# A three-block network on one core: two row homes for the scan, weights split in place, and the weight load waits for the matmuls

## The chip, the cores and the metric

The kernel runs on one core of a Trainium2 chip. Its time is the device time of one execution in microseconds (us). Before the change three timed runs gave 2862.00, 2860.92 and 2841.12 us (median 2860.92 us), and the one profiled execution took 2826.98 us with a span of 2825.3 us.

## The reference, cut to what matters

One sequence of 512 tokens, width 1024, float32, goes through two layers of a first block and one of a second:

```python
x = layer_norm(ALPHA * x + even_mixer(x)); x = layer_norm(ALPHA * x + conv_ffn(x))   # retention + stick-breaking
x = layer_norm(ALPHA * x + odd_mixer(x));  x = layer_norm(ALPHA * x + conv_ffn(x))   # differential attention
x = x + hybrid_mixer(rms_norm(x))             # SSD scan + windowed attention, gated
x = x + memory_cross_attention(rms_norm(x), rms_norm(mem))
x = x + swiglu_ffn(rms_norm(x)); return rms_norm(x)
...
def ssd_chunked(xh, dt, a_head, b_in, c_in):  # the scan, here for both directions and 32 heads
    a_cum = cumsum(dt * a_head)
    decay = exp(where(lower, a_cum[:, :, :, None] - a_cum[:, :, None], -inf))
    cb = einsum('bclgn,bcsgn->bclsg', c_c, b_c)
    y_diag = einsum('bclsg,bclsgr,bcsgrp->bclgrp', cb, decay, x_c)
    ... # plus what earlier chunks hand on
```

The kernel computes the scan as full 512 by 512 products: for each head the decay weights exp(row - column) times C·B, times the tokens.

## The kernel before, in words

**Weights.** All weight matrices lie in memory as one stream of 405 units, each 128 partitions of 8 blocks of 128 float32 (512 KB). Every matmul of a weight is done in three parts for accuracy: high part of the weight by high and low part of the activation, low part of the weight by the high one. One unit is 48 matmuls of 256 columns in `product_tile` (L338), or the same work in `half_tile` (L369) and the memory products (L1467). A unit passes through a ring of four slots (RING = 4) in three tensors. SP loads it into `w_raw` (`load_unit`, L305). ScalarE copies it into `w_hi`, which rounds (`split_hi`, L313). VectorE writes `w_lo` = `w_raw` - `w_hi` (`split_lo`, L319). Unit u uses slot u mod 4. PE waits for `lo_done` and counts `units_used` when it is done with a unit. `split_hi` of unit u+4 waits for `units_used` of unit u. The load of unit u+4 waits only for `lo_done` of unit u, since `w_raw` is then free: the raw copy lies ready long before PE gives the slot back.

**The engines' order.** Every engine runs its program in the order written. ScalarE's program says, tile for tile: wait until PE is done with the tile, evict it from PSUM, then `split_hi` of the unit four ahead. VectorE likewise has its `split_lo` between evictions and norms. Nothing reorders this when a wait is long. PSUM has two banks for product tiles (`acc`), so PE can start a tile only when the tile two before it is evicted.

**The scan** (`ssd_pe`, `ssd_act`, `ssd_dve`, `ssd_rows_dma`; stage `ssd`). 16 head tiles f, in 4 groups g of 4 (j = 0 to 3). For a tile PE computes two product tiles (gate and x, L338), then the heads of the tile before (L1731, L1734: 16 matmuls with the decay weights as the moving side), then transposes of x (L1769). At j = 0 it also makes C·B (L1752), at j = 1 a sum of squares (L1740). The decay weights of two heads (b = 0, 1) are 5 slots of 2 KB each: GpSimd fills them from `scratch_rows` by eight broadcast DMAs of 320 KB (L1710), one per chunk c and head, each after PE is done with that chunk of the previous tile (`s_pv`). VectorE caps a chunk (L1867), ScalarE takes the exponentials (L1842), VectorE multiplies by C·B (L1872), PE uses it. There is one home of 10 slots for these rows, so tile f+1's rows start only after tile f's heads. ScalarE waits for the transposes before it starts on the exponentials (L1831 ahead of L1842), and VectorE does both `split_lo` and the output (L1879, L1882) before the first cap.

**Layer norms beside matmuls.** After `even_out`, `down0` and `odd_out` the norm is done in halves of 256 columns: while PE does the last tiles in halves (L369), ScalarE's `tail_act` first does one `split_hi` and then the squares (L460), whose sum PE takes (L453). In other places a stage's end is: evict the last tile, `split_hi`, then the work on which PE waits (copies of transposes L677, L1152, L2051, the last square L1327, the high parts L2220).

## Time and profile before

| | |
|---|---|
| timed runs | 2862.00, 2860.92, 2841.12 us (median 2860.92) |
| the profiled execution's own time | 2826.98 us |
| its span | 2825.3 us |
| PE busy | 2647.1 us (94%) |
| VectorE busy | 1453.8 us (51%) |
| ScalarE busy | 1244.8 us (44%) |
| scan, the stretch from 1540 to 1870 us | 330 us |

A busy time is the time in which an engine had an instruction under way. It is an average over stages with different limits, so the windows by stage and the waits tell more than the shares. The chain of waits is followed back from the last instruction. A number in brackets behind an instruction is the idle time of its engine just before it, and what ended it. Matmul records overlap, since matmuls are pipelined.

### The profile page before, as it was taken

The page shows a single profiled execution, that of the slowest core. Times are in us where ns is not written, and L with a number is a line of the kernel's source. Part 1 is how long each engine was busy: PE and PEld are TensorE (multiplying, and loading weights), DVE is VectorE, ACT ScalarE, POOL GpSimd, SP SyncE. Part 2 cuts the span into 40 slices and gives each one's busy share as a digit, 9 for nine tenths or more (in the row PEclk, how much of TensorE's full clock was granted, in tenths as well). Part 3 has the DMA queues.
Part 4 walks back from the last instruction along what each step waited for, and adds up shares of the span by engine and source line. Part 5 has one row for each costly group of instructions (what it writes and reads, how often), then busy time and mean ns, then how long its engine had stood idle before and what let it go on. Part 6 is the DMA issues. An engine that isn't in the chain of part 4 may idle for free.

```text
span 2825.3 us, 52535 instructions
## 1 busy us (share of the span) xinstructions
PE 2647.1 (94%) x20916; PEld 2429.6 (86%) x20916; DVE 1453.8 (51%) x2514; ACT 1244.8 (44%) x2045; POOL 83.5 (3%) x157
## 2 busy tenths in 40 slices
PE   7998999999998699999988999889988998999998
PEld 7985899999996399999987776679966986899998
DVE  3233476553424766664466777752376343433333
ACT  3335354432425644442355777752465234333321
POOL 0000000000000000000001211200000000000000
PEclk9999999999999999999999999999999999999999
DMA  6310122222321022223253454532211231222231
GB/s 181 123 67 0 45 90 89 95 98 99 112 97 53 1 75 99 95 98 119 98 187 117 169 197 156 186 123 98 89 46 53 97 105 45 75 97 97 97 105 68
DMA packets 74693, 278.20 MB, mean 98 GB/s; under 512 B 9642, under 2 KB 9674, under 8 KB 74048
## 3 DMA queue, kind: packets, MB, share of 16 engines
q1 hardware_dynamic: 60816, 217.42, 22.4%
q0 software_dynamic: 13744, 58.88, 6.8%
q8 instruction: 98, 1.61, 0.2%
q14 instruction: 35, 0.29, 0.0%
HBM read 267.03 MB, written 9.24 MB: 98 GB/s over the span
## 4 chain that ended last, share of the span: by engine, by line
PE 79%; DVE 9%; ACT 5%; DMA 4%; issue 3%; DVEq 0%; ACTq 0%; POOL 0%; POOLq 0%; SPq 0%
PE acc L338 66%; PE acc L369 2%; DMA res_tmp<-scratch_rows 2%; PE ps L813 1%; DMA w_raw<-in_stream 1%; PE ps L369 1%; PE acc L1467 1%; ACT w_hi L313 1%; PE ps L453 1%; DVE big L2173 1%; DVE big L1276 1%; PE ps L1740 1%; PE acc L827 1%; DVE res_tmp L1872 1%; DVE res_tmp L1358 1%
## 5 line engine op out<-in xcount | busy, mean ns | idle before, releaser
L338 PE MATMUL acc<-x_split,w_hi 128*128 128x256 f32 x7968 | 1254.6, 280 | 23.6 <-DVE x_split L1363 12.0
L338 PEld LDWEIGHTS acc<-x_split,w_hi 128*128 128x128 f32 x7968 | 1072.3, 190 | 28.6 <-issue 22.2
L319 DVE TENSOR_TENSOR w_lo<-w_raw,w_hi 128x1024 fp32r<-128x1024 f32 x405 | 493.1, 1222 | 605.9 <-ACT w_hi L313 605.9
L338 PE MATMUL acc<-x_split,w_lo 128*128 128x256 f32 x3984 | 786.3, 279 | 0.0
L313 ACT ACTIVATE w_hi<-w_raw 128x1024 fp32r<-128x1024 f32 x405 | 424.9, 1054 | 578.8 <-PE acc L338 527.2
L338 PEld LDWEIGHTS acc<-x_split,w_lo 128*128 128x128 f32 x3984 | 609.1, 190 | 0.0
L338 PE MATMUL acc<-big_r,w_hi 128*128 128x256 f32 x3560 | 559.0, 279 | 7.7 <-DVE big_r L2226 3.4
L338 PEld LDWEIGHTS acc<-big_r,w_hi 128*128 128x128 f32 x3560 | 477.5, 188 | 9.8 <-issue 3.6
L338 PE MATMUL acc<-big_r,w_lo 128*128 128x256 f32 x1780 | 351.7, 279 | 0.0
L338 PEld LDWEIGHTS acc<-big_r,w_lo 128*128 128x128 f32 x1780 | 271.6, 189 | 0.0
L1842 ACT ACTIVATE res_tmp<-res_tmp 128x512 f32<-128x512 f32 (+3 forms) x256 | 120.7, 550 | 43.4 <-DVE res_tmp L1867 42.9
L958 ACT ACTIVATE res_tmp<-acc,par 128x512 f32<-128x512 f32 x84 | 64.8, 772 | 143.0 <-PE acc L338 138.5
L983 DVE SCALAR_TENSOR_TENSOR res_tmp<-acc,par,res_tmp 128x511 f32<-128x511 f32 x84 | 62.9, 748 | 93.5 <-ACT res_tmp L958 93.2
L1872 DVE TENSOR_TENSOR res_tmp<-res_tmp 128x640 f32<-128x640 f32 x128 | 99.0, 819 | 6.6 <-ACT res_tmp L1842 5.9
L1602 DVE SCALAR_TENSOR_TENSOR big<-acc,par,big 128x510 f32<-128x510 f32 (+3 forms) x96 | 71.9, 749 | 37.7 <-ACT big L1592 27.9
L1710 POOL DMA_DIRECT2D res_tmp<-scratch_rows x128 | 68.7, 537 | 295.4 <-PE ps L1734 227.0
L986 DVE SCALAR_TENSOR_TENSOR res_tmp<-acc,par,res_tmp 128x510 f32<-128x510 f32 x84 | 62.9, 748 | 13.1 <-DVE res_tmp L983 3.1
L963 ACT ACTIVATE res_tmp<-res_tmp 128x512 f32<-128x512 f32 x44 | 27.8, 633 | 89.5 <-DVE small L991 89.5
L1120 ACT ACTIVATE big<-acc 128x512 f32 (+1 forms) x30 | 18.0, 599 | 109.5 <-PE acc L338 107.1
L369 PE MATMUL acc<-big_r,w_hi 128*128 128x256 f32 x344 | 61.9, 283 | 0.5 <-DVE res_tmp L533 0.5
L1867 DVE TENSOR_TENSOR res_tmp<-res_tmp 128x512 f32<-128x512 f32 x64 | 43.3, 687 | 31.9 <-DMA res_tmp<-scratch_rows 31.9
L1731 PE MATMUL ps<-res_tmp,big 128*64 128x512 f32 (+3 forms) x256 | 48.2, 455 | 10.3 <-DVE res_tmp L1872 10.1
(291 smaller groups left out, 2579.1 us busy)
## 6 DMA issues: line engine op xcount, KB each, us to landing
w_raw<-in_stream SPq DMA_DIRECT2D x405, 512.0 KB, 3.3
res_tmp<-scratch_rows POOLq DMA_DIRECT2D x128, 320.0 KB, 5.7
scratch_bias<-res_tmp POOLq DMA_DIRECT2D x1, 2560.0 KB, 55.3
res_tmp<-in_x SPq DMA_DIRECT2D x2, 1024.0 KB, 7.7
res_tmp<-scratch_bias POOLq DMA_DIRECT2D x8, 256.0 KB, 4.4
scratch_x<-res_tmp POOLq DMA_DIRECT2D x1, 2048.0 KB, 8.1
scratch_kv<-big POOLq DMA_DIRECT2D x1, 2048.0 KB, 8.7
res_tmp<-scratch_x POOLq DMA_DIRECT2D x1, 2048.0 KB, 8.5
```

What stands on the lines that cost most here:

```text
L313: act.activation(w_hi[:, u.slot], w_raw[:, u.slot], ACT.Copy).then_inc(hi_done, 1)
L319: dve.tensor_tensor(w_lo[:, u.slot], w_raw[:, u.slot], w_hi[:, u.slot].bitcast(F32), ALU.subtract).then_inc(lo_done, 1)
L338: mm = pe.matmul(a[:, h], w, AR[:, x + k, h], start=(k == 0 and w is wh and x == hi and h.start == 0), stop=(k == total - 1 and w is wl), ...
L369: mm = pe.matmul(a[:, cols], w, AR[:, x + k, cols], start=(start and k == 0 and w is wh and x == hi), stop=(k == total - 1 and w is wl), s ...
L958: act.activation(x, acc[t.bank][:], ACT.Identity, bias=col(f"cb{f}", tile), scale=col(f"cw{f}", tile + 88)).then_inc(ev("conv_now"), 1)
L983: dve.scalar_tensor_tensor(x[:, 1:S], a[:, 0:S - 1], col(f"cw{f}", tile + 44), x[:, 1:S], ALU.mult, ALU.add).then_inc(ev("conv_tap1"), 1)
L986: dve.scalar_tensor_tensor(x[:, 2:S], a[:, 0:S - 2], col(f"cw{f}", tile), x[:, 2:S], ALU.mult, ALU.add).then_inc(acc_free[t.bank], 1)
L1602: ins = dve.scalar_tensor_tensor(o, i, col("cw2", m + 24 * j), o, ALU.mult, ALU.add)
L1710: pool.dma_start(part(b, c), src).then_inc(ev(f"s_row_in{b}{c}"), 16)
L1731: pe.matmul(o(b, c * P, S), x(b, c), rows_buf(b)[:, FORE[c]:FORE[c] + LEN[c]], start=(c == 0), stop=False, skip_group_check=True)
L1842: ins = act.activation(x, x, ACT.Exp, bias=tab[:, 0, c, ds(head, 1)])
L1872: dve.tensor_tensor(w, w, cb, ALU.mult).then_inc(ev("s_w"), 1)
```

## The change

Three things change together.

1. `w_raw` is given the address of `w_lo`: VectorE's subtraction writes the low part over the raw unit. So the load of unit u+4 may no longer start when the low part of unit u is made; it waits for `units_used`, that is until PE is done with unit u. The three ring tensors of 16 KB each per partition become two. The arena before them grows from 76 to 84 slots of 2 KB, by just the 16 KB, so `w_hi` and `w_lo` keep their addresses.
2. The scan's rows get two homes of 10 slots (`rows_buf(p, b)`), for even and odd tiles, and `s_pv` starts 8 higher: the rows of tile f+2 are loaded when the heads of tile f are done, chunk by chunk.
3. Inside the scan VectorE caps the first two chunks before the output of the tile before, and spreads the two `split_lo` and the `times_cb` between the other caps. ScalarE starts the exponentials at once and copies the transposed x (L1831) after the first two chunks.

```diff
-RES = 60
-TMP = 68
-N_SLOTS = 76
+RES = 64
+TMP = 72
+N_SLOTS = 84
...
-        w_raw = ctx.enter_context(nc.sbuf_tensor("w_raw", [P, RING, BLK * P], F32))
         w_hi = ctx.enter_context(nc.sbuf_tensor("w_hi", [P, RING, BLK * P], F32R))
+
+        home = nc.sbuf_base
         w_lo = ctx.enter_context(nc.sbuf_tensor("w_lo", [P, RING, BLK * P], F32R))
+        w_raw = nc.alloc_sbuf_tensor_at("w_raw", [P, RING, BLK * P], F32, offset=home)
...
         def load_unit(sp, u, wait=True):
             if wait:
-                sp.wait_ge(lo_done, (u + (-RING)).count + 1)
+                sp.wait_ge(units_used, (u + (-RING)).count + 1)
...
             def body(i):
-                for c in range(CH):
-                    for b in range(2):
-                        pool.wait_ge(ev("s_pv"), 8 * i + (2 * c + b + 1))
-                        src = SCR_ROWS[ds(2 * i + b, 1), BACK[c]:BACK[c] + S + P].to_broadcast([P, S + P])
-                        pool.dma_start(part(b, c), src).then_inc(ev(f"s_row_in{b}{c}"), 16)
-            repeat(pool, SSD_TILES, body)
+                for p in range(2):
+                    for c in range(CH):
+                        for b in range(2):
+                            pool.wait_ge(ev("s_pv"), 16 * i + (8 * p + 2 * c + b + 1))
+                            src = SCR_ROWS[ds(4 * i + (2 * p + b), 1), BACK[c]:BACK[c] + S + P].to_broadcast([P, S + P])
+                            pool.dma_start(part(p, b, c), src).then_inc(ev(f"s_row_in{p}{c}"), 16)
+            repeat(pool, SSD_TILES // 2, body)
...
-                    act.wait_ge(ev("s_xtt"), f + 1)
-                    act.activation(A[:, XTOK + j % 2], ps[:, 2], ACT.Copy).then_inc(ev("s_xtok"), 1)
                     table_of_exp_and_ln(act)
                     if j == 1 and not first:
                         rstd(g + (-1))
                     for c in range(CH):
+                        if c == 2:
+                            act.wait_ge(ev("s_xtt"), f + 1)
+                            act.activation(A[:, XTOK + j % 2], ps[:, 2], ACT.Copy).then_inc(ev("s_xtok"), 1)
...
-            dve.memset(small[:, 41:42], 0.0).then_inc(ev("s_pv"), 2 * CH)
+            dve.memset(small[:, 41:42], 0.0).then_inc(ev("s_pv"), 4 * CH)
...
+                    cap(g, j, 0)
+                    cap(g, j, 1)
+                    if j or not first:
+                        out(4 * g + (j - 1), (j - 1) % 4)
                     split_lo(dve, uz + RING)
-                    split_lo(dve, uz + 1 + RING)
...
+                    cap(g, j, 2)
+                    times_cb(f, j, 0)
+                    split_lo(dve, uz + 1 + RING)
+                    cap(g, j, 3)
+                    times_cb(f, j, 1)
...
+                    times_cb(f, j, 2)
+                    times_cb(f, j, 3)
```

Lines below the ring tensors move: L305 becomes L307, L313 L315, L319 L321, L1602 L1606, L1867 L1873, L1872 L1879, L1879 L1886, L1882 L1889, L1831 L1841 and L1842 L1848.

**SP's queue, the loop that loads the stream**, with the semaphore that each row waits for. Before:

```order
L305 ISA [waits w_lo_done]
L305 DMA w_raw<-in_stream 128x1024
L302 REGISTER_ALU
L305 ISA [waits w_lo_done]
L305 DMA w_raw<-in_stream 128x1024
```

Now:

```order
L307 ISA [waits w_units_used]
L307 DMA w_raw<-in_stream 128x1024
L304 REGISTER_ALU
L307 ISA [waits w_units_used]
L307 DMA w_raw<-in_stream 128x1024
```

Nothing moves in this queue; each load waits for the matmuls in place of the subtraction.

**VectorE, one tile of the scan** (second tile of the first group, from its convolution to the next one's; `big` are the arena's lower slots, `res_tmp` its upper ones). Before:

```order
L1602 SCALAR_TENSOR_TENSOR big<-acc,par,big 128x510
L319 TENSOR_TENSOR w_lo<-w_raw,w_hi 128x1024 x2
L1879 SCALAR_TENSOR_TENSOR big<-big,par,ps 128x512
L1882 TENSOR_TENSOR big<-big 128x512
L1867 TENSOR_TENSOR res_tmp<-res_tmp 128x2x256 x2
L1872 TENSOR_TENSOR res_tmp<-res_tmp 128x640 x2
L1867 TENSOR_TENSOR res_tmp<-res_tmp 128x2x256
L1872 TENSOR_TENSOR res_tmp<-res_tmp 128x640 x2
L1867 TENSOR_TENSOR res_tmp<-res_tmp 128x2x256
L1872 TENSOR_TENSOR res_tmp<-res_tmp 128x640 x4
```

Now:

```order
L1606 SCALAR_TENSOR_TENSOR big<-acc,par,big 128x510
L1873 TENSOR_TENSOR res_tmp<-res_tmp,big 128x2x256 x2
L1886 SCALAR_TENSOR_TENSOR big<-big,par,ps 128x512
L1889 TENSOR_TENSOR big<-big 128x512
L321 TENSOR_TENSOR w_lo<-w_raw,w_hi 128x1024
L1873 TENSOR_TENSOR res_tmp<-res_tmp,big 128x2x256
L1879 TENSOR_TENSOR res_tmp<-res_tmp,big 128x640 x2
L321 TENSOR_TENSOR w_lo<-w_raw,w_hi 128x1024
L1873 TENSOR_TENSOR res_tmp<-res_tmp,big 128x2x256
L1879 TENSOR_TENSOR res_tmp<-res_tmp,big 128x640 x6
```

The same instructions in number: two caps stand ahead of the output, and the second low part stands behind the first products with C·B.

**ScalarE, the same tile.** Before:

```order
L1592 ACTIVATE big<-acc,par 128x512
L1821 ACT_TABLE_LOAD
L1821 ACTIVATE big<-acc 128x512
L313 ACTIVATE w_hi<-w_raw 128x1024 x2
L1827 ACTIVATE big<-big 128x512
L1831 ACTIVATE big<-ps 128x512
L285 ACT_TABLE_LOAD
L1842 ACTIVATE res_tmp<-res_tmp 128x512
```

Now:

```order
L1596 ACTIVATE big<-acc,par 128x512
L1826 ACT_TABLE_LOAD
L1826 ACTIVATE big<-acc 128x512
L315 ACTIVATE w_hi<-w_raw 128x1024 x2
L1832 ACTIVATE big<-big 128x512
L287 ACT_TABLE_LOAD
L1848 ACTIVATE res_tmp<-res_tmp,big 128x512
```

The copy of the transposed x (L1831) has gone from between the activation of x and the exponentials; it now stands eight exponentials later. The two `split_hi` stay where they were, ahead of the activation of x (L1827) for which PE's transposes wait.

## Rows read from the trace of the kernel before

**Rows 1.** The page: span, and PE's busy time with its share.

```profile
span 2825.3 us, 52535 instructions
PE 2647.1 (94%) x20916; PEld 2429.6 (86%) x20916; DVE 1453.8 (51%) x2514; ACT 1244.8 (44%) x2045; POOL 83.5 (3%) x157
```

**Rows 2.** The scan's stretch: busy us of PE, PEld, DVE, ACT, POOL; clock, DMA share, GB/s.

```profile
1540.00:1870.00 330.00, 289.13 (x2080) 226.59 (x2078) 263.40 (x376) 257.01 (x446) 67.34 (x126) 0.94 0.52 178
```

**Rows 3.** Waits in the scan, 1540 to 1871: us in total, times, longest.

```profile
DVE res_tmp L1867 <- DMA res_tmp<-scratch_rows: 31.9, 21, 3.2
PE ps L1769 <- ACT big L1827: 25.6, 13, 3.4
```

**Rows 4.** The chain of waits, 1763 to 1803: start, us, what.

```profile
1769.39 11.09 PE acc L338 x96
1780.48 3.43 PE ps L1752 x8
...
1790.81 9.45 DMA res_tmp<-scratch_rows
```

**Rows 5.** Instructions of PE in order of time, 1762 to 1781: start, us, engine, line.

```profile
1763.34 1.08 PE L1731 MATMUL ps<-res_tmp,big 128*64 128x512 f32 x4
...
1768.74 0.66 PE L1769 MATMUL ps<-const,big 128*128 128x128 f32 x4 [0.87 <-ACT big L1827]
```

**Rows 6.** Instructions of VectorE in order of time, 1822 to 1885.

```profile
1827.93 3.43 DVE L1602 SCALAR_TENSOR_TENSOR big<-acc,par,big 128x510 f32<-128x510 f32 x4 [0.44 <-ACT big L1592]
...
1846.83 3.43 DVE L1602 SCALAR_TENSOR_TENSOR big<-acc,par,big 128x510 f32<-128x510 f32 x4
```

**Rows 7.** The page's groups: the two splits; busy us, mean ns; idle before, releaser.

```profile
L319 DVE TENSOR_TENSOR w_lo<-w_raw,w_hi 128x1024 fp32r<-128x1024 f32 x405 | 493.1, 1222 | 605.9 <-ACT w_hi L313 605.9
...
L313 ACT ACTIVATE w_hi<-w_raw 128x1024 fp32r<-128x1024 f32 x405 | 424.9, 1054 | 578.8 <-PE acc L338 527.2
```

**Rows 8.** The page's DMA issues: count, KB each, median us to landing.

```profile
w_raw<-in_stream SPq DMA_DIRECT2D x405, 512.0 KB, 3.3
...
scratch_bias<-res_tmp POOLq DMA_DIRECT2D x1, 2560.0 KB, 55.3
```

**Rows 9.** The weight loads issued in 34 to 60 us: issues, and time to landing.

```profile
L305 SPq DMA_DIRECT2D w_raw<-in_stream x4: 332/333/333, 39.6 to 55.8; - x4
...
DMA to landing us min/median/max: 22.8/26.0/27.8
```

**Rows 10.** Instructions of ScalarE in order of time, 20 to 90.

```profile
51.27 0.60 ACT L623 ACTIVATE res_tmp<-acc 64x512 f32<-64x512 f32 x1 [3.15 <-PE acc L338]
...
62.45 1.06 ACT L313 ACTIVATE w_hi<-w_raw 128x1024 fp32r<-128x1024 f32 x1 [4.54 <-DMA w_raw<-in_stream]
...
69.92 1.06 ACT L313 ACTIVATE w_hi<-w_raw 128x1024 fp32r<-128x1024 f32 x1 [5.18 <-DMA w_raw<-in_stream]
```

**Rows 11.** Instructions of ScalarE at stage ends, 184 to 190 and 2441 to 2446.

```profile
184.80 1.05 ACT L313 ACTIVATE w_hi<-w_raw 128x1024 fp32r<-128x1024 f32 x1
185.74 4.01 ACT L677 ACTIVATE big<-ps 128x512 f32<-128x512 f32 x8
...
2444.02 1.06 ACT L313 ACTIVATE w_hi<-w_raw 128x1024 fp32r<-128x1024 f32 x1 [4.07 <-PE acc L338]
```

**Rows 12.** ScalarE in the norm after `even_out`, 342 to 351.

```profile
342.64 1.06 ACT L313 ACTIVATE w_hi<-w_raw 128x1024 fp32r<-128x1024 f32 x1 [12.20 <-PE acc L369]
343.90 2.73 ACT L460 ACTIVATE res_tmp<-res_tmp 128x256 f32<-128x256 f32 x8 [0.20 <-DVE res_tmp L478]
```

**Rows 13.** VectorE at the end of `even_out`, 328 to 334.

```profile
329.18 1.23 DVE L319 TENSOR_TENSOR w_lo<-w_raw,w_hi 128x1024 fp32r<-128x1024 f32 x1 [0.47 <-ACT w_hi L313]
...
333.33 0.41 DVE L533 SCALAR_TENSOR_TENSOR res_tmp<-res_tmp,acc 128x256 f32<-128x256 f32 x1
```

**Rows 14.** VectorE in `up1`, one pair of tiles, 1127 to 1134.

```profile
1127.21 1.22 DVE L319 TENSOR_TENSOR w_lo<-w_raw,w_hi 128x1024 fp32r<-128x1024 f32 x1
...
1132.42 0.75 DVE L986 SCALAR_TENSOR_TENSOR res_tmp<-acc,par,res_tmp 128x510 f32<-128x510 f32 x1
```

More of the change, by code:

```diff
@@ L1624, in bcdt_act @@
             act.activation(d, d, ACT.Ln).then_inc(ev("s_logdt"), 1)
-            rows = rows_buf(0)
+            rows = rows_buf(0, 0)
             act.wait_ge(ev("s_rows"), 8)
@@ L1668, in bcdt_dve @@
             split_lo(dve, u + RING)
-            rows = rows_buf(0)
+            rows = rows_buf(0, 0)
             dve.wait_ge(ev("s_ones"), 1)
@@ L1696, in ssd_rows_dma @@
         def ssd_rows_dma(pool):
-            rows = rows_buf(0)
+            rows = rows_buf(0, 0)
             pool.wait_ge(ev("s_rows"), 8)
@@ L1853, in ssd_dve, with cap @@
             dve.wait_ge(ev("s_tab"), 2)
-            dve.memset(small[:, 41:42], 0.0).then_inc(ev("s_pv"), 2 * CH)
+            dve.memset(small[:, 41:42], 0.0).then_inc(ev("s_pv"), 4 * CH)
             dve.memset(small[:, 42:43], 0.0).then_inc(ev("s_w"), 1)
-            def cap(f, head, c):
-                for b in range(2):
-                    dve.wait_ge(ev(f"s_row_in{b}{c}"), 16 * (f + 1))
-                x = A[:, ROWS:ROWS + 10].rearrange("p (b m) n -> p b (m n)", b=2)
+            def cap(g, j, c):
+                p, head = j % 2, g * 8 + 2 * j
+                dve.wait_ge(ev(f"s_row_in{p}{c}"), 64 * g + 32 * (j // 2 + 1))
+                x = A[:, ROWS + 10 * p:ROWS + 10 * p + 10].rearrange("p (b m) n -> p b (m n)", b=2)
                 x = x[:, :, (S + 2 * P) * c:(S + 2 * P) * c + 2 * P].rearrange("p b (k n) -> p b k n", k=2)
@@ L1867, in cap, with times_cb @@
                 dve.tensor_tensor(x, x, own, ALU.min).then_inc(ev("s_cap"), 1)
-            def times_cb(f, b, c):
-                dve.wait_ge(ev("s_e"), 8 * f + (2 * c + b + 1))
-                w, cb = part(b, c), cb_packed[:, BACK[c]:BACK[c] + S + P]
-                dve.tensor_tensor(w, w, cb, ALU.mult).then_inc(ev("s_w"), 1)
+            def times_cb(f, j, c):
+                for b in range(2):
+                    dve.wait_ge(ev("s_e"), 8 * f + (2 * c + b + 1))
+                    w, cb = part(j % 2, b, c), cb_packed[:, BACK[c]:BACK[c] + S + P]
+                    dve.tensor_tensor(w, w, cb, ALU.mult).then_inc(ev("s_w"), 1)
             def out(f, j):
                 v = A.at(VL, f)
-                dve.wait_ge(ev("s_pv"), 8 * f + 4 * CH)
+                dve.wait_ge(ev("s_pv"), 8 * f + 6 * CH)
                 dve.wait_ge(ev("s_xt"), f + 1)
@@ L1910, in group @@
                     uz, tz = Units(UB["ssd"] + 2 * j, g, 8), Tiles(TB["ssd"] + 2 * j, g, 8)
-                    x = A[:, XT + j % 2]
-                    conv5_dve(dve, tz + 1, f + 8, f + 8, x)
+                    conv5_dve(dve, tz + 1, f + 8, f + 8, A[:, XT + j % 2])
                     if j == 0:
                         table_diagonals(g)
+                    cap(g, j, 0)
+                    cap(g, j, 1)
+                    if j or not first:
+                        out(4 * g + (j - 1), (j - 1) % 4)
                     split_lo(dve, uz + RING)
-                    split_lo(dve, uz + 1 + RING)
                     if j == 2 and not first:
                         scaled(g + (-1))
-                    if j or not first:
-                        out(4 * g + (j - 1), (j - 1) % 4)
                     if j == 0:
@@ L1923, in group @@
                         dve.wait_ge(ev("s_cb_rest"), 4 * g + 4)
+                    cap(g, j, 2)
[3 more added lines that the diff above has]
+                    times_cb(f, j, 1)
                     if j == 3 and not first:
                         lows(g + (-1))
-                    for c in range(CH + 1):
-                        if c < CH:
-                            cap(f, g * 8 + 2 * j, c)
-                        if c:
-                            times_cb(f, 0, c - 1)
-                            times_cb(f, 1, c - 1)
+                    times_cb(f, j, 2)
+                    times_cb(f, j, 3)
             group(0, True)
@@ L1953, in gated_act @@
             if not first:
-                act.wait_ge(ev("s_pv"), 2 * CH * (SSD_TILES + 1))
+                act.wait_ge(ev("s_pv"), 2 * CH * (SSD_TILES + 2))
             per = 1 + len(blocks)
```

19 lines of the change are left out of this document (10 added, 9 removed).

## The prediction

> **What bounds the kernel now.** I read the page first: PE is busy 94% of a span of 2825.3 us [rows 1], so on the whole time goes only when PE stops, and the three other engines matter where they make it stop. Next the stretch of the scan, because the change names it: there PE is busy 289 of 330 us, at 0.94 of the full clock, while VectorE has 263 and ScalarE 257 us of work [rows 2]. So 41 us of PE's idle time lie there, and no other engine is near its limit on average. The waits say who makes the others idle: VectorE's cap waited 31.9 us for the decay rows, and PE's transposes waited 25.6 us in 13 waits for ScalarE's activation of x [rows 3]. The chain of waits shows the loop: products of 11.09 us, C·B of 3.43 us, then the heads, and after these 9.45 us of row DMA before VectorE may start [rows 4]. With one home the rows of a tile can't come before the heads of the tile before.
>
> Then I looked at what hides the weight loads. The raw copy lands 3.3 us after issue in the median [rows 8]. The splits take 1.05 and 1.22 us, and the page's rows say for whom they waited: `w_hi` in 527.2 of its 578.8 us for PE, to give the slot back; its waits for a load are too small to be named first [rows 7]. The reader is to see in this that ScalarE stands at PE's heels: at stage ends `split_hi` starts at once behind the eviction, and the next work of ScalarE starts at once behind it [rows 11].
>
> **The change part by part.** The sum is made against the profiled execution.
>
> *Nothing by itself:* no instruction is added to PE, VectorE or ScalarE. The arena grows by 16 KB, just what the third ring tensor took, so the weights that PE reads stand at the same addresses. Writing the low part over the raw unit is the same instruction, and I see no row by which an equal output address costs; it is read and written by one engine in step. I price it at 0.
>
> *The rows in two homes.* Their DMA (9.45 us in the chain) goes behind a whole tile of other work: it starts with the heads of tile f and is wanted 17 us later. What is late next? PE's own tile: 11.09 us of products [rows 4], then from the first head at 1763.34 to the end of the transposes at 1768.74 + 0.66 is 6.06 us, with 0.87 us of waiting in it for ScalarE [rows 5]. That is 17.15 us a tile; a group of four has 3.43 us of C·B and as much for the sum of squares on top: 4 x 17.15 + 6.9 = 75.5 us. VectorE, which ran without a gap there, took 1846.83 - 1827.93 = 18.9 us for a tile in which it scales a group, and has about as much in the tile with the low parts [rows 6]; the new order puts no work away, so in two tiles of four it holds PE up by about 1 us each. So 77.5 us a group, 310 us for four against 330 us: **-20 us**. Bounds: at best all 41 us of idle time and a clock back from 0.94 (some 14 us more), -55 us; at worst the second `split_hi` of each tile waits for a load whose slot was given back only 2.6 us earlier, 16 tiles at 1 to 2 us, and half of the gain is gone: -5 us. I take the middle since the floor comes from rows of this very loop.
>
> *The load waits for PE.* From "PE done with unit u" to "raw copy of u+4 there" now pass the 3.3 us of [rows 8] and some 0.2 us for SP, 3.5 us in place of nothing. In a plain stage that is hidden: a unit takes PE 5.4 us, the slot is wanted again after three units (16 us), and 3.5 + 1.05 + 1.22 us fit. But ScalarE now stands in `split_hi` for up to 3.5 us with everything behind it queued, and VectorE behind ScalarE in `split_lo`. I went through each stage end:
> - Four times the copies of transposed tiles stand behind the last `split_hi` of a stage (184.8, 878.1, 2074.6 and 2354.7). The slot came free 0.6 us before the split started, so each is 2.9 us later [rows 11]: 4 x 2.9 = 11.6 us.
> - Two rms norms (2300.3 and 2444.0) have the last square behind a `split_hi` that starts at once when PE stops [rows 11]: 2 x 3.5 = 7 us.
> - Before `mix_out`, before `bcdt` and within it (2251.4, 1463.2, 1474) the split stands ahead of high parts, low parts and scans: 3.2 + 3.2 + 1.5 = 7.9 us.
> - The halved norms. At the end of `even_out` VectorE's split at 329.18 stands ahead of the half tile's eviction at 333.33, and PE waited for that one already [rows 13]: 3.5 us. Then `split_hi` at 342.64 stands ahead of the squares at 343.90, which PE takes as they come [rows 12]: the load lands at 346.1, the split ends at 347.1, 3.2 us later. `odd_out` is the same code, `down0` has only the second: 2 x 6.7 + 3.1 = 16.5 us.
> - The cross attention's keys (`xkv`) are half as wide, 2.8 us a unit, between two norms, and a 2 MB store runs beside them. ScalarE is often 2 to 5 us behind there, which hides part: 5 us, between 0 and 10.
>
> Together **+48 us**. The lower bound: where a load lands while ScalarE is late anyway, it costs nothing; half of it, 24 us. Above: each new stop of PE may be followed by a stretch at a lower clock, as the scan's 0.94 shows for its stops, 1 us at 12 places, 60 us.
>
> *The start.* Early in the first stage a DMA of 2560 KB is under way for 55.3 us [rows 8], and four weight loads issued from 39.6 to 55.8 us took 22.8 to 27.8 us [rows 9]. Before, that was covered, since units 4 to 7 had been loaded ahead of it: of ScalarE's waits for loads of 4.5 and 5.2 us [rows 10] PE felt about 2 us. Now unit 4 is asked for when PE is done with unit 0, at about 35 us (51.27 us is the fourth tile's eviction, 5.44 us a tile back), and lands at 35 + 22.8 = 58 us. Meanwhile ScalarE stands in `split_hi`, the second tile isn't evicted, and PE stops after the third, at 46 us, until 61 us. The next loads land 69.92 - 62.45 = 7.5 us apart [rows 10], slower than PE's 5.44 us, until the DMA is over; by then PE is at unit 7 at 94 us. Unit 9 ends at 105 us in place of 35 + 9 x 5.44 + 2 = 86 us: **+19 us**.
>
> Weighed against this: the Trainium skill (DMA: Bandwidth & Descriptors, Queues, rings and completion order) says that a DMA engine goes round robin between its queues, packet by packet. By that a load would pass the big DMA at every second packet and come in perhaps 8 us, and the start would cost 3 us, the sum be 16 us less. The trace disagrees for the first load (22.8 us with nothing ahead of it in its own queue) and is nearer to it for the next (7.5 us apart). I go by the rows and keep 3 us as the lower bound; the upper one is 26 us, with 27.8 us for the first landing.
>
> The same skill page (Rules for kernel authors) advises to issue a DMA early and wait for it late, since its fixed cost is then hidden. It speaks against this change: the load is issued as late as it can be. That is the +48 us above, which rests on the rows and not on the rule.
>
> *A margin to watch.* In `up0` and `up1` a pair's second split ends, and 1132.42 + 0.75 - (1127.21 + 1.22) = 4.7 us later the next tile's bank is free [rows 14]. With the load behind PE that split ends at 5.44 + 0.1 + 3.5 + 1.05 + 1.22 = 11.3 us after the pair's first tile, so the bank is free at 16.0 us, and PE wants it at 3 x 5.44 = 16.3 us. 0.3 us is left: I price it at 0, and it is a rival.
>
> **Sum:** -20 + 48 + 19 = +47 us. The profiled execution's 2827 us becomes 2874 us. It lies 34 us below the median of the timed runs, and the runs before spread over 21 us; the differences are per stage and not tied to what changes, so I add the sum to the median: 2861 + 47 = **2908 us**.
>
> **The rivals.**
> 1. *The late loads land in the shade of late engines* (not slower; chance 0.05). If ScalarE came to its split 3.5 us after PE gave the slot back, neither it nor PE would notice. Then the stage ends cost nothing, the start 3 us, and the scan brings 35 us: 2861 - 32 = 2829 us. It decides at a lateness of 3.5 us. For it: in the scan and `xkv` ScalarE is that late. Against it: at the stage ends it starts within 0.6 us [rows 11].
> 2. *Half in the shade* (within 1%; chance 0.20). The stage ends cost 24 us, the start 8 us, the scan brings 20 us: 2861 + 12 = 2873 us.
> 3. *The conv stages lose their margin* (chance 0.10). If landings vary by 0.5 us more than the 0.3 us left, each of 44 pairs costs 0.5 us: 22 us more, 2930 us. The median landing of 3.3 us speaks against it; a spread above 3.6 us would be for it.
> 4. *The change is not what it says* for addresses: were the weights moved relative to the 2 KB grid, PE's spacing could change in all stages. The sizes say no (8 x 2048 = 4 x 1024 x 4 bytes); less than 0.01.
>
> **How the numbers follow.** A measurement of this kernel can tell about 1% (28.6 us) from no change: below 2832 us is faster, above 2889.5 us slower. The forecast has 0.65. Its own range from the bounds of its terms is 2861 + (24 + 3 - 55) to 2861 + (60 + 26 - 5), with the ends not all together 2882 to 2930. Rival 2 lies in the middle band, rival 3 above, rival 1 at the lower edge, most of it beyond. Slower: 0.65 less 0.03 for its lower tail, and 0.10, is 0.72 plus the upper part of rival 2, 0.02: 0.74. Within 1%: 0.22. Faster: 0.04. To leave out no more than 2 in 10 the range takes in most of rival 2 and rival 3: 2866 to 2936 us.
>
> **What would show it.** In the profile after, `w_hi`'s idle time should have the load as a large releaser (hundreds of us), and SP should wait for PE. Loads should land 3.3 us after issue in plain stages with PE unbroken. At 187.7 us (plus the start's 19) the split should start 3.5 us after PE's end, and L677 behind it. PE should stop at about 46 us for 15 us. The scan should take about 310 us, with VectorE's wait for the rows gone and PE's for the activation of x still there or larger. It would be wrong if the scan's stretch shrinks by 35 us or more, or if PE's stops at the stage ends are no longer than before.

## The result and the profile after

The changed kernel took 2891.59, 2898.46, 2898.55 and 2907.14 us (median 2898.5), the kernel before beside it 2840.64 to 2862.0 us (median 2851.0). The ratio is 1.0214, with a 95% interval of 1.0166 to 1.0263: slower. Between the four runs of each the medians differ by 47.5 us (1.0167, the lower end of that interval); by the ratio it is some 61 us, and the changed kernel measured once more, in six runs beside ten, is 63.5 us slower by medians (last experiment). So the change costs about 60 us. A run more than 1.5% above the fastest of its kernel is left out of the ratios: one of the twelve of late_in_scan below took 6001.18 us, and one of the kernel before 2859.47 us. The forecast was 2908 us, which is 47 us more than its 2861. The side and most mechanisms came out as forecast, but three terms did not have their size, and one cause of the scan's gain was not seen at all.

The page of the profile after: span and busy times; the two splits with the idle time before them; the DMA issues with their median time to landing.

```profile
span 2889.9 us, 52449 instructions
PE 2668.3 (92%) x20916; PEld 2446.6 (85%) x20916; DVE 1451.7 (50%) x2514; ACT 1261.3 (44%) x2045; POOL 83.8 (3%) x157
...
L321 DVE TENSOR_TENSOR w_lo<-w_raw,w_hi 128x1024 fp32r<-128x1024 f32 x405 | 495.1, 1223 | 968.0 <-ACT w_hi L315 967.4
L315 ACT ACTIVATE w_hi<-w_raw 128x1024 fp32r<-128x1024 f32 x405 | 427.0, 1059 | 1049.4 <-DMA w_raw<-in_stream 1049.0
...
w_raw<-in_stream SPq DMA_DIRECT2D x405, 512.0 KB, 3.3
res_tmp<-scratch_rows POOLq DMA_DIRECT2D x128, 320.0 KB, 5.6
scratch_bias<-res_tmp POOLq DMA_DIRECT2D x1, 2560.0 KB, 54.4
```

Against [rows 1, 7, 8]: the span grew by 64.6 us, PE's busy time by 21 us. The load still lands in 3.3 us, and both splits last as long as before. But `split_hi`, which had waited 527.2 us for PE, now waits 1049.0 us for the load. The next line is SP's waits (us in total, times, longest): it now stands behind PE, as the new wait says.

```profile
SPq L307 <- PE acc L340: 2387.5, 362, 131.6
```

Where the time went is read from the stretches of single stages, which go by the kernel's names (`UB` and `STAGES` at its top): `even_out` and `odd_out` hold a mixer's attention and its last products, `mix_out` the last products of the third mixer, `up0`, `up1` and `ffn_in` are the wide feed-forward products, `down0` and `ffn_out` the ones behind them, `xkv` and `xq` belong to the cross attention, and `bcdt` stands just ahead of the scan. PE's idle time in a stage is its length less PE's busy time. Here are two stages of the kernel before, and then the same two of the changed one (first stage and `even_out`; columns as in [rows 2]).

```profile
20.00:184.20 164.20, 159.27 (x1358) 156.35 (x1358) 53.65 (x63) 51.45 (x69) 1.69 (x2) 0.97 0.45 121
184.20:355.30 171.10, 155.18 (x806) 111.88 (x807) 74.62 (x162) 74.74 (x89) 0.00 (x0) 0.97 0.07 23
```

```profile
20.00:208.50 188.50, 165.02 (x1358) 162.03 (x1358) 53.32 (x63) 53.71 (x69) 1.70 (x2) 0.91 0.38 98
208.50:389.20 180.70, 157.54 (x807) 112.92 (x807) 75.19 (x163) 74.67 (x89) 0.00 (x0) 0.96 0.07 24
```

Read the same way for all stages:

| | before: length, PE idle | after | repeated run of after |
|---|---|---|---|
| first stage (`even_in`) | 164.2, 4.9 | 188.5, 23.5 | 189.5, 24.4 |
| scan (`ssd`) | 318.1, 31.4 | 288.4, 14.1 | 288.3, 14.9 |
| all others | 2311.0, 117.2 | 2381.0, 159.2 | 2395.0, 155.8 |

So the start cost 24 us, the scan brought 30 us, and the other stages grew by 70 us, 42 of them idle time of PE. All stages together are 64.6 us longer.

**The start.** The instructions of ScalarE, and then of PE, in order of time.

```profile
59.14 1.06 ACT L315 ACTIVATE w_hi<-w_raw 128x1024 fp32r<-128x1024 f32 x1 [21.87 <-DMA w_raw<-in_stream]
60.22 0.59 ACT L625 ACTIVATE res_tmp<-acc 64x512 f32<-64x512 f32 x1
66.59 1.06 ACT L315 ACTIVATE w_hi<-w_raw 128x1024 fp32r<-128x1024 f32 x1 [5.18 <-DMA w_raw<-in_stream]
```

```profile
62.19 1.22 PE L340 MATMUL acc<-x_split,w_hi 128*128 128x256 f32 x4 [15.28 <-DVE big L653]
...
86.95 0.73 PE L340 MATMUL acc<-x_split,w_hi 128*128 128x256 f32 x4 [4.10 <-DVE big L653]
```

The reader is to see the forecast's chain: the load lands, the split runs, the eviction (L625) stood behind it, and PE, idle since 46.9 us, goes on after 15.28 us. What the forecast did not price is the start after the stop: these first matmuls take 1.22 us for four, and from 62.19 to 67.5 us, 5.3 us long, the granted clock is 0.50, the lower level of 1.2 GHz, where the kernel before had 1.00 (45 to 65 us).

**A stage's end.** ScalarE after the last tile of the first stage, to be held against [rows 11]; then two stretches of PE's heads behind it (L699), before and after.

```profile
208.66 0.60 ACT L637 ACTIVATE big<-acc 128x512 f32 x1 [0.99 <-PE acc L340]
211.99 1.06 ACT L315 ACTIVATE w_hi<-w_raw 128x1024 fp32r<-128x1024 f32 x1 [2.73 <-DMA w_raw<-in_stream]
212.95 4.00 ACT L679 ACTIVATE big<-ps 128x512 f32<-128x512 f32 x8
```

```profile
189.80:194.40 4.60, 4.59 (x17) 3.01 (x18) 1.69 (x4) 1.25 (x1) 0.00 (x0) 1.00 0.02 6
```

```profile
217.00:223.30 6.30, 6.30 (x17) 3.96 (x18) 1.68 (x4) 1.25 (x1) 0.00 (x0) 0.73 0.01 3
```

The split waits 2.73 us where it had started at once, and the copies stand behind it. Then the same 17 matmuls take 6.3 us in place of 4.6, at a clock of 0.73 and not 1.00: PE's longer wait was followed by slower matmuls. All fourteen profiles agree at this place. In six of them 5.8 to 5.9 us pass from the start of PE's last product matmul to the first of these heads, and the 17 matmuls run at 1.00; in the other eight 8.6 to 8.9 us pass, and they run at 0.59 to 0.74. This stop cost 5.0 us in all, of which the forecast had 2.9.

**The scan.** The stretch that answers to [rows 2], the waits that answer to [rows 3], and the chain of waits.

```profile
1609.30:1909.60 300.30, 276.73 (x2077) 217.56 (x2078) 260.93 (x379) 255.75 (x447) 68.89 (x128) 0.98 0.58 194
```

```profile
PE ps L1774 <- ACT big L1832: 15.0, 12, 2.9
...
DVE res_tmp L1873 <- DMA res_tmp<-scratch_rows: 4.3, 3, 2.4
```

```profile
1651.87 10.91 PE acc L340 x96
...
1668.61 10.90 PE acc L340 x96
1679.50 3.43 PE ps L1757 x8
...
1687.98 10.89 PE acc L340 x96
1698.87 3.43 PE ps L1745 x8
...
1707.35 10.91 PE acc L340 x96
```

300 us in place of 330. The wait for rows fell from 31.9 to 4.3 us, and no row DMA is left in this chain. The tiles of this chain take 16.74 us, those with C·B or the sum of squares 19.4 us. In the last two groups two tiles of four take 0.7 to 2 us more than that; PE's waits in two of these tiles, 1.9 and 0.7 us, are for ScalarE's activation of x. The clock is back from 0.94 to 0.98. PE's wait for the activation of x became smaller (15.0 for 25.6 us).

### The profile page after: what moved, and what is told of

Same layout as the page of the kernel before. It is cut to its first block, busy times and chain, and to the rows that moved or that the text cites. A ratio compares the mean times of both kernels' runs of the same rounds, so it can differ in the third digit from the quotient of the medians.

```text
span 2889.9 us, 52449 instructions
## 1 busy us (share of the span) xinstructions
PE 2668.3 (92%) x20916; PEld 2446.6 (85%) x20916; DVE 1451.7 (50%) x2514; ACT 1261.3 (44%) x2045; POOL 83.8 (3%) x157
## 4 chain that ended last, share of the span: by engine, by line
PE 77%; DVE 10%; ACT 5%; DMA 4%; issue 3%; DVEq 0%; SPq 0%; ACTq 0%
PE acc L340 65%; DMA w_raw<-in_stream 4%; PE acc L371 2%; PE ps L815 1%; ACT w_hi L315 1%; DVE w_lo L321 1%; DVE res_tmp L1879 1%; DVE big L1606 1%; PE acc L1469 1%; DVE big L2181 1%; DVE big L1278 1%; PE ps L455 1%; PE ps L371 1%; PE acc L829 1%; DVE res_tmp L1360 1%
## 5 line engine op out<-in xcount | busy, mean ns | idle before, releaser
L340 PE MATMUL acc<-x_split,w_hi 128*128 128x256 f32 x7968 | 1260.3, 281 | 51.3 <-DVE big L653 20.6
L321 DVE TENSOR_TENSOR w_lo<-w_raw,w_hi 128x1024 fp32r<-128x1024 f32 x405 | 495.1, 1223 | 968.0 <-ACT w_hi L315 967.4
L315 ACT ACTIVATE w_hi<-w_raw 128x1024 fp32r<-128x1024 f32 x405 | 427.0, 1059 | 1049.4 <-DMA w_raw<-in_stream 1049.0
L340 PEld LDWEIGHTS acc<-big_r,w_hi 128*128 128x128 f32 x3560 | 480.4, 190 | 14.4 <-issue 6.7
L1848 ACT ACTIVATE res_tmp<-res_tmp,big 128x512 f32<-128x512 f32 (+3 forms) x256 | 120.3, 552 | 11.8 <-DVE res_tmp L1873 11.6
L1879 DVE TENSOR_TENSOR res_tmp<-res_tmp,big 128x640 f32<-128x640 f32 x128 | 97.3, 816 | 2.3 <-ACT res_tmp L1848 2.0
L1606 DVE SCALAR_TENSOR_TENSOR big<-acc,par,big 128x510 f32<-128x510 f32 (+3 forms) x96 | 71.8, 748 | 35.8 <-ACT big L1596 25.9
L371 PE MATMUL acc<-big_r,w_hi 128*128 128x256 f32 x344 | 62.9, 286 | 7.2 <-DVE res_tmp L535 7.2
L988 DVE SCALAR_TENSOR_TENSOR res_tmp<-acc,par,res_tmp 128x510 f32<-128x510 f32 x84 | 62.9, 748 | 13.1 <-DVE res_tmp L985 3.1
L371 PEld LDWEIGHTS acc<-big_r,w_hi 128*128 128x128 f32 x344 | 53.9, 193 | 7.9 <-DVE res_tmp L535 7.6
L1469 PE MATMUL acc<-x_split,w_hi 128*128 128x256 f32 x256 | 47.9, 290 | 8.4 <-ACT big L1476 8.4
```

What stands on the lines that cost most here:

```text
L315: act.activation(w_hi[:, u.slot], w_raw[:, u.slot], ACT.Copy).then_inc(hi_done, 1)
L321: dve.tensor_tensor(w_lo[:, u.slot], w_raw[:, u.slot], w_hi[:, u.slot].bitcast(F32), ALU.subtract).then_inc(lo_done, 1)
L340: mm = pe.matmul(a[:, h], w, AR[:, x + k, h], start=(k == 0 and w is wh and x == hi and h.start == 0), stop=(k == total - 1 and w is wl), ...
L371: mm = pe.matmul(a[:, cols], w, AR[:, x + k, cols], start=(start and k == 0 and w is wh and x == hi), stop=(k == total - 1 and w is wl), s ...
L988: dve.scalar_tensor_tensor(x[:, 2:S], a[:, 0:S - 2], col(f"cw{f}", tile), x[:, 2:S], ALU.mult, ALU.add).then_inc(acc_free[t.bank], 1)
L1469: mm = pe.matmul(acc[t.bank][:, 0:MEM], w, mem_r(x, k), start=(k == 0 and w is wh and x == MEM_H), stop=(k == KD - 1 and w is wl))
```

## The experiments

Each ratio is to the kernel before on the same chip, with its 95% interval.

### One part alone: late_load

```diff
-                sp.wait_ge(lo_done, (u + (-RING)).count + 1)
+                sp.wait_ge(units_used, (u + (-RING)).count + 1)
```

> The kernel before with one line changed: the load of unit u+4 waits until PE is done with unit u; w_raw keeps its own 16 KB, the scan is as before. Theory (the load's latency costs, as forecast): the profile after shows 43 us more of idle PE in all, although the scan's idle time fell by 17 us; with the clock lost after the stops this should be 60 to 80 us slower than before, about 2851 + 70 = 2921 us, and the rows show PE's stop of 15 us at about 46 us. Rival (writing the low part over the raw unit is what costs, the wait is hidden): no change, 2851 us within 10.

Measured: 1.0278 (1.0239 to 1.0318), median 2909.4 against 2833.2 us. The wait alone costs more than the whole change. PE's stop at the start is there (first stage 188.6 us), and outside the scan each stage's idle time of PE is within 1.0 us of the changed kernel's. But the scan's stage took 298.3 us, and it has one home and the old order: 20 of the 30 us came without the homes.

### The address: in_place

```diff
-        w_raw = ctx.enter_context(nc.sbuf_tensor("w_raw", [P, RING, BLK * P], F32))
...
+        home = nc.sbuf_base
         w_lo = ctx.enter_context(nc.sbuf_tensor("w_lo", [P, RING, BLK * P], F32R))
+        w_raw = nc.alloc_sbuf_tensor_at("w_raw", [P, RING, BLK * P], F32, offset=home)
```

> As late_load, and w_raw takes the address of w_lo (the arena grows by 8 unused slots, so w_hi and w_lo keep their addresses); the scan is as before. Theory: the same time as late_load within 6 us, and split_lo still takes 1.22 us, since the instruction is the same. Rival (an equal output and input address costs): late_load is at 2851 us and this one at 2921 us, or split_lo is longer than 1.25 us.

Measured: 1.0282 (1.0244 to 1.0320), `split_lo` 1224 ns in both. Writing over the raw unit costs nothing that can be measured, as forecast.

### The order inside the scan: homes_old_order

```diff
-                    cap(g, j, 0)
-                    cap(g, j, 1)
-                    if j or not first:
-                        out(4 * g + (j - 1), (j - 1) % 4)
                     split_lo(dve, uz + RING)
+                    split_lo(dve, uz + 1 + RING)
...
+                    if j or not first:
+                        out(4 * g + (j - 1), (j - 1) % 4)
```

> The changed kernel with its two row homes, but inside the scan VectorE and ScalarE keep the order of the kernel before (both low parts and the output ahead of the caps; the copy of the transposed x ahead of the exponentials). Theory 1 (the second home brings the gain, the order little): at most 8 us slower than the changed kernel, about 2898 + 5 = 2903 us. Theory 2 (the order carries half or more of the 30 us that the scan's stage gained): 15 to 25 us slower, about 2918 us, with PE waiting in the heads for VectorE's products with C·B.

Measured: 1.0219 (1.0171 to 1.0267); the scan's stage 291.2 us for 288.4. Theory 1 holds: the order (ScalarE's copy of the transposed x is put back too) is worth 3 us in the profile and nothing that the timed runs can show.

### Who hits whom in the scan: late_in_scan

```diff
+                sp.wait_ge(units_used if scan else lo_done, (u + (-RING)).count + 1)
...
+            for lo, hi, scan in ((1, 59, False), (59, 66, True), (66, N_UNITS // RING, False)):
```

> The kernel before with one home and the old order, but the loads of units 236 to 263, which belong to the scan, wait until PE is done with the unit four earlier; all other loads wait for the low part as before. Theory C, formed from late_load (its scan's stage took 298.3 us and not 318.1, though it has one home): two weight loads no longer start in the middle of the eight row DMAs. The scan's stage gets 15 to 20 us shorter and the kernel 0.6% faster than before, ratio 0.994, since no other stage is touched. Rival D (the shorter stage in late_load came with the state of PE's clock in that execution, or only because the stages ahead of it were late): ratio 1.000 within 0.3%, and the weight loads in the scan still land after about 8 us.

Measured: 0.9943 (0.9909 to 0.9976), faster than both kernels. The scan's stage in the kernel before: DMA issues (count, KB, median us to landing), then the stretch.

```profile
res_tmp<-scratch_rows POOLq DMA_DIRECT2D x120, 320.0 KB, 5.7
w_raw<-in_stream SPq DMA_DIRECT2D x32, 512.0 KB, 8.0
```

```profile
1527.60:1845.70 318.10, 286.70 (x2110) 231.81 (x2112) 248.36 (x359) 248.45 (x429) 64.41 (x120) 0.96 0.51 177
```

The same of late_in_scan, with VectorE's wait for rows between them.

```profile
res_tmp<-scratch_rows POOLq DMA_DIRECT2D x120, 320.0 KB, 5.4
w_raw<-in_stream SPq DMA_DIRECT2D x32, 512.0 KB, 3.3
```

```profile
DVE res_tmp L1867 <- DMA res_tmp<-scratch_rows: 15.9, 18, 2.2
```

```profile
1530.90:1828.20 297.30, 277.90 (x2111) 226.25 (x2112) 246.58 (x356) 246.52 (x425) 64.41 (x120) 0.98 0.55 186
```

In the kernel before both low parts of a tile are made just after the heads, so their two 512 KB loads (issued at 1769.2 and 1770.4 us in one tile) ran beside the eight row DMAs of 320 KB (issued 1765.3 to 1770.0). The loads took 8.0 us in the median, a row DMA up to 10.2 us, and VectorE waited 31.9 us for rows. When the loads wait for PE they start in the product tiles: 3.3 us, at most 7.2 us for a row DMA, and 15.9 us of waiting. The chain of waits has seven row DMAs over this stage in either kernel, 62.9 us before and 41.5 us now. One of before and two of late_in_scan (start, us):

```profile
1604.09 10.16 DMA res_tmp<-scratch_rows
```

```profile
1624.29 6.99 DMA res_tmp<-scratch_rows
1700.89 6.36 DMA res_tmp<-scratch_rows
```

Theory C stands: this one delay takes 21 us out of the chain and 21 us off the stage. No other stage pays in idle time of PE (117.6 us for 117.2 outside start and scan); in this one profile they are 7 us longer, 3.2 of them in `even_out` at a clock of 0.94 for 0.97, where the two kernels do the same.

### Two homes with early loads: raw_two_early

`w_raw` with two slots in place of four frees 8 KB, room for a second home of two chunks.

```diff
+RAW = 2
...
+                sp.wait_ge(lo_done, (u + (-RAW)).count + 1)
...
+        def home(p, c):
+            return p if c < 2 else 0
```

> As raw_two_homes (w_raw with two slots, a second home for two of four chunks, the changed order in the scan), but the loads of the scan wait only for the low part of two units before, so they start beside the row DMAs again. It is the fourth corner of one home or two, loads late or early: the scan's stage took 318 us (one, early), 298 us (one, late), 290 us (two, late). Theory E (late loads and the second home are substitutes: both take the same wait for rows off the path): scan's stage 290 to 295 us, ratio like raw_two_homes, 1.003. Theory F (they add up, each worth its own part): about 310 us, ratio 1.009.

Measured: 1.0025 (0.9991 to 1.0059), as theory E had it; the start takes back what the scan gains (189.3 us for 164.2, for the reason given in the next section). The scan's stage here: the loads, VectorE's wait for rows, the stretch.

```profile
w_raw<-in_stream SPq DMA_DIRECT2D x32, 512.0 KB, 7.4
```

```profile
DVE res_tmp L1885 <- DMA res_tmp<-scratch_rows: 2.0, 4, 0.7
```

```profile
1549.40:1839.50 290.10, 277.19 (x2110) 225.97 (x2110) 245.25 (x357) 246.68 (x427) 66.57 (x124) 0.98 0.58 199
```

The loads still meet the rows (7.4 us), but VectorE hardly waits for the rows (2.0 us for 31.9). That is the fourth corner:

| scan's stage, us | loads early | loads late |
|---|---|---|
| one home | 318.1 | 298.3, 299.2, 298.9, 297.3 |
| second home | 290.1 | 288.3 to 292.5 |

Theory E: they are substitutes. Homes alone bring 28 us, late loads alone 19 to 21, both together 26 to 30. The corners are not quite alike: this second home holds two chunks of four, it comes with the changed order (3 us by homes_old_order), and the 318.1 us are one profile.

### Both gains: raw_two_homes

The same with the scan's loads waiting for PE as well.

> A version meant to have both gains: w_raw, w_hi and w_lo apart, but w_raw with two slots in place of four (the load of unit u+2 waits for the low part of unit u), which frees 8 KB; there two chunks of the scan's rows get a second home, the other two keep one; VectorE and ScalarE in about the changed kernel's order; the loads of the scan wait for PE too, as in late_in_scan. Theory: two raw slots hide a load of 3.3 us behind a unit of 5.4 us, so all stages but the scan take what they took before, and the scan's stage about 290 us in place of 318: ratio 0.990. Rival (two slots are too few: at stage ends or at the start the second split waits): the scan's gain is eaten, ratio 1.000 or more.

Measured: 1.0026 (0.9989 to 1.0062); the expectation failed, and its rival held. The scan's stage took 290.4 us, but the first stage 187.8: with two raw slots unit 6 is asked for only when the 2560 KB are under way (it landed after 23.0 us), and PE waited 16.0 us for VectorE's evictions at the start. `xkv` and `bcdt` grew by 4 us each.

### The start: after_bias_late, after_bias_vt, late_not_start

```diff
+            pool.wait_ge(units_used, 28)
             pool.dma_start(SCR_BIAS, row).then_inc(ev("bias_out"), 16)
```

> The changed kernel, but the DMA of 2560 KB to scratch_bias waits until PE is done with unit 27, the end of the first stage, where no weight load is under way. Theory (that DMA delays the loads of units 4 to 9): their landings fall from up to 27 us to about 4 us, PE's stop at 46.9 us goes, and the kernel is 20 us faster than the changed one, about 2878 us; a remainder of 2 to 4 us may stay since the first tiles come while ScalarE still has its start work. Rival (the first loads are slow by themselves or wait in their own queue): landings stay over 15 us and the time within 4 us of 2898.

Measured: 1.0280 (1.0240 to 1.0320), so no faster. Yet the first stage fell to 163.2 us and no load in 30 to 90 us took over 4.1 us: that DMA is what delayed them. The 25 us were lost, and 14 more, in the next stage, 219.8 us for 180.7. I took the loads of units 29 to 31 for the cause there, and wrote the next kernel on it (the same wait, on the transposed tiles' `ev_vtok` in place of `units_used`):

> The changed kernel, with the DMA of 2560 KB issued only when all eight transposed tiles after the first stage have been copied; the kernel after_bias_late issued it 5 us earlier, and there PE stood idle for 33 us more in the stage even_out, because the loads of units 29 to 31 and that DMA ran together and ScalarE stood in the split ahead of those copies. Theory: now no load that ScalarE waits for meets it until unit 28 is used in even_out, the first stage takes 163 us, even_out 181 us, and the kernel is 20 to 25 us faster than the changed one: ratio to before 1.0214 - 0.008 = 1.013. Rival (the 2560 KB slow the attention or hit the first loads of even_out, so the time only moves again): ratio 1.020 or more.

Measured: 1.0327 (1.0280 to 1.0373), worse, with 66 us of idle PE in `even_out`. My cause was wrong: the weight loads there land in 3.2 us. ScalarE's row in after_bias_late names it.

```profile
237.76 1.08 ACT L742 ACTIVATE res_tmp<-acc 128x512 f32<-128x512 f32 x2 [44.87 <-DMA scratch_bias<-res_tmp]
```

The 2560 KB are read from two slots of `res_tmp` that L742 writes, and it waits for `bias_out` before it does. The DMA can't go there unless its source moves. So the start was measured the other way round, with loads 4 to 23 early:

```diff
+            with sp.Fori(1, 6) as i:
+                for j in range(RING):
+                    load_unit(sp, Units(j, i, RING), late=False)
```

> As late_load (kernel before, every load waits for PE), but the loads of units 4 to 23 wait for the low part as before, so the start is untouched. Theory (in late_load 24 us of the first stage's growth come from units 4 to 8 being asked for while the 2560 KB are under way): the first stage takes 165 us again, and the ratio to the kernel before falls from 1.028 to 1.028 - 0.0085 = 1.0195. Rival (the lost time only moves to the next stages): ratio 1.026 or more.

Measured: 1.0205 (1.0160 to 1.0250), against late_load's 1.0278, as expected. The first stage, in late_load and then here:

```profile
20.00:208.60 188.60, 164.81 (x1358) 161.83 (x1358) 53.57 (x63) 53.75 (x70) 1.70 (x2) 0.91 0.37 98
```

```profile
20.00:184.40 164.40, 159.47 (x1358) 156.50 (x1358) 53.41 (x63) 52.30 (x70) 1.69 (x2) 0.97 0.42 108
```

24 us, of which 18.9 are PE's idle time and 5.3 its longer busy time at a clock of 0.91.

### Stage ends: splits_behind

```diff
+        LATE = [UB["even_out"] + 3, UB["odd_out"] + 3, UB["qkv"] + 15, UB["xq"] + 11]
...
-            if isinstance(u.count, int) and u.count >= N_UNITS:
+            if isinstance(u.count, int) and (u.count >= N_UNITS or (u.count in LATE and not now)):
```

> The changed kernel, but at four stage ends (before the transposes of even_in, odd_in, qkv and xq) ScalarE copies the transposed tiles first and does the last split_hi behind them. Theory (ScalarE's queue stands behind the late load there): the four stops of PE get shorter by what they had grown, 5.0 + 4.0 + 2.4 + 3.7 = 15 us, so ratio to the kernel before about 1.0214 - 0.0053 = 1.016. Rival (PE's stops there grew through something else, such as the lower clock after the stop or the copies themselves): ratio as for the changed kernel, 1.021.

Measured: 1.0221 (1.0174 to 1.0268): no gain that the timed runs can show, and the expected 1.016 lies outside the interval. In the trace the mechanism is there:

```profile
910.29 0.60 ACT L1124 ACTIVATE big<-acc 128x512 f32<-128x512 f32 x1 [0.46 <-PE acc L342]
911.70 4.03 ACT L1156 ACTIVATE big<-ps 128x512 f32<-128x512 f32 x8 [0.81 <-PE ps L1150]
915.53 1.13 ACT L317 ACTIVATE w_hi<-w_raw 128x1024 fp32r<-128x1024 f32 x1
```

The copies no longer wait for the load, and the split finds it landed. From the end of PE's last product tile before the attention to the end of its first one behind, the four places are shorter by 3.5, 2.8, 1.1 and 3.2 us, 10.6 of the expected 15. But `even_out` as a whole is only 1.1 us shorter, with 4.3 us less idle and 3.2 us more busy time at a clock of 0.93 for 0.96. The lower clock isn't behind this stop, where the 17 matmuls take 4.6 us at 1.00 again, but elsewhere in the stage. Executions differ by as much there: the kernel before and late_in_scan do the same up to the scan, and in `even_out` PE is busy 155.2 us at 0.97 in one and 160.0 us at 0.94 in the other. So it stays open whether the 3.2 us belong to the edit.

### A version with both: both_raw

```diff
+        w_sep = nc.alloc_sbuf_tensor_at("w_sep", [P, RING, BLK * P], F32, offset=base + 76 * S * 4)
...
+        def raw(u):
+            return (w_raw if 233 <= u.base < 289 else w_sep)[:, u.slot]
```

> A version meant to beat both: two full row homes and the changed order in the scan, the low part written over the raw unit and the load behind PE for units 233 to 288 (scan and the stage after it) alone; for all other units w_raw lies apart and is loaded early. The 16 KB of that separate w_raw hold most of the second row home while the scan runs. Theory: scan's stage 288 to 290 us as in the changed kernel, all others as before, so 2793 - 30 = 2765 us in the stages and a ratio of 0.990, a little below late_in_scan (0.9943). Rival (the 7 to 10 us between 298 and 288 us are lost again at the switch between the two ways of loading): ratio 0.995 or more.

Measured: 0.9935 (0.9903 to 0.9967), median 2805.8 against 2830.0 us: faster than before and after. It lies between the expected 0.990 and the rival's 0.995, and within its interval it is the same as late_in_scan, which needs only the other wait. The scan's stage took 291.4 us; the 6 us against late_in_scan are below what the timed runs tell.

### The changed kernel once more: after_again

> The changed kernel once more, unchanged, to set its ratio (1.0214 from four runs each) beside those of the experiments, which have six to twelve runs, and to see which parts of its profile repeat. If the 21 us by which PE's busy time in the profile grew are mostly the spacing of its matmuls, which changes from one execution to the next, idle time by stage repeats within 2 us and the length of ffn_in, ffn_out and up1 does not; the ratio lies between 1.017 and 1.026. Against it: a ratio above 1.026, which would make the second home worth nothing beside late_load's 1.028.

Measured: 1.0203 (1.0149 to 1.0258). PE's idle time is 195.1 us for 196.8, and by stage within 2 us. The spacing I expected to differ did so in other stages: a unit of 48 matmuls takes PE either 5.44 or 5.65 us, for long stretches, and which stages have 5.65 changes (`even_out`, `odd_in`, `mix_out` and `xq` in this run, not in the first; `ffn_in` and `up1` in both). 124 units were of the slow kind in the kernel before, 148 and 185 in the two executions after, but 112 in late_load, so on the whole the late load does not bring it: 0.21 us each, 5 and 13 us of the profiles' difference. One stage is an exception. In `up1` (44 units) none is of the slow kind in the five profiles with early loads there, and 22 to 37 are in each of the nine with late loads. That is some 5 to 8 us by which the late load may lengthen `up1` without a stop; no run separates the two.

## Why the prediction was right, point by point

- **What bounds it.** Right: PE's stops set the time, and `split_hi` at PE's heels passes a late load on to PE at once.
- **Nothing by itself.** Right: in_place equals late_load.
- **The scan, -20 us.** Measured -30. The step failed twice. The floor of 77.5 us a group was too high: the groups took 72 to 75 us (the first, with no heads before it, 66), since a plain tile took 16.74 and not 17.15 us, C·B and the sum of squares added 2.6 and not 3.4 us each, and the clock rose from 0.94 to 0.98. The 2 us a group for a late engine did come in the last two groups, but PE's waits there were for ScalarE and not for VectorE. And the prediction looked at the row DMAs alone: it saw 9.45 us in [rows 4] and never asked what else was on the DMA queues at that time. So it missed that the change's own later loads (its part 1) free the rows of two competitors. For the changed kernel this makes next to no difference, because the homes cover the wait in any case (290.1 with early, 290.4 us with late loads, with half a second home).
- **The load waits for PE, +48 us.** The places were right. The stops themselves came to 42 us of PE's idle time outside start and scan, a little under the sum, but those stages grew by 70 us: 28 us of longer busy time stood in the sum at nothing. By ratios late_not_start to late_in_scan is 1.0205/0.9943, 2.6% or some 75 us, with about 16 us either way. At `even_out` the three places named took 5.0 + 3.0 + 1.6 = 9.6 us and 9.6 were forecast; at `odd_out` 10.6; the two rms norms 4.3 us each for 3.5; `mix_out` 4.5 for 3.2; `xkv` 6.3 for 5. Of the 28 us some 5 are the spacing of the matmuls. Most of the rest goes with the lower clock (0.73 at 217 us; mean 0.972 for 0.982), which the forecast had only in its upper bound; how much of it the stops bring and how much changes between executions is not separated.
- **The start, +19 us.** Mechanism and stop as forecast (15.28 us for 15), 24 us in all; 18.6 of them are idle, and 5.8 us of busy time at a lower clock were left out. The forecast had weighed the Trainium skill (DMA: Bandwidth & Descriptors, Queues, rings and completion order), by whose turn-taking between queues the start would cost 3 us. These runs decide for the row: the first three loads landed after 22.9 to 26.9 us, and of the next three one took 13.2 us.
- **The margin in `up0` and `up1`, priced 0.** It held but for one stop: each of the two stages has 2 to 2.7 us more of idle PE, nearly all in one stop early in the stage (2.4 us at 430 us, 2.0 us in `up1`), where PE waited for the bank that the margin is about. Rival 3 did not come; `up1` grew by 8.9 us, but 2.0 of them are idle and some 5 are the slower spacing.
- **Rivals 1 and 2** needed loads in the shade of late engines. That was so nowhere but in the scan.
- **What would show it.** All came but two: the scan took 300 us for the 310 named, and PE's wait for the activation of x fell.

The sum was less right than the time. It had +47 us, and the stages of the profile say 64.6, the ratio 61 and the second measurement 63.5: the scan brought 10 us more than forecast, the start cost 5 us more and the other stages 22 us more. That these errors had opposite signs is luck. So is most of the hit in microseconds, 2908 for 2898.5: the forecast stood on a median of 2861 us, and the kernel before had 2851 us beside the changed one.

## What to carry to other kernels

A load that waits for the consumer costs its latency only where an in-order engine stands behind it: go through each stage's end and the program's start, and add the slower matmuls after each stop to the stop. Where a stage waits for DMAs, list every DMA issued in the same few microseconds: to issue a load later, in that stage alone, brought 21 us for no memory, where the second home of 20 KB with it brought 30. And two remedies for one wait do not add up.

## What the runs showed of the hardware

- After a stop of 15.28 us PE's granted clock was 0.50 for the first 5.3 us. At the end of the first stage, where PE had waited 2.3 us and shortly before 1.4 us, it was 0.73 over the next 6.3 us. There the cost of a stop was more than its length.
- A 512 KB load takes 3.3 us alone, 8.0 us beside eight DMAs of 320 KB, and 22.9 us when a DMA of 2560 KB was under way ahead of it.
- Matmuls of one form run at two spacings, 5.44 or 5.65 us a unit at a granted clock of 1.00 in both, for whole stages; it changes between executions of one kernel. `ffn_out` took 119.7 us before and 124.4 us after by it alone, with no idle time in either. What sets it stays open.
